# Scores of two heads issued together, behind transposes and values, in a two-layer attention trunk

## What is computed

```python
def _fox_attention(...):       # 16 heads of 64
    for i in range(S // 128):
        s = q[lo:hi] @ k[:hi].T * scale + (c[lo:hi, None] - c[None, :hi])
        p = softmax(where(causal, s, NEG_INF))
        out = p @ v[:hi]
def _dilated_group(q, k, v, window, dilation):   # (128,1), (512,4), (2048,16), 16 heads each
    s = where(mask, q @ k.T * scale, NEG_INF)
    m = max(s); p = exp(s - m); den = sum(p)
    return (p / den) @ v, m + log(den)
# merged: softmax over the three groups' m + log(den)
```

## Time and profile before

| | us |
|---|---|
| median of 3 runs | 1691.82 (1689.79 to 1691.88) |
| span of the profiled execution | 1690.7 |
| TensorE matmul busy | 1670.5 (99%) |
| weight loads busy | 1393.1 (82%) |
| VectorE busy | 811.6 (48%) |
| ScalarE busy | 598.7 (35%) |
| GpSimd busy | 359.3 (21%) |
| scores (L515), 512 instructions | 125.3 |

### The profile page before, as it was taken

How to read it: one execution, slowest core, us unless ns; L and a number is a source line. 1 busy time by engine, 2 the same in 40 slices (tenths; PEclk the granted TensorE clock), 3 DMA queues, 4 the chain that set the end, 5 groups by cost and what they waited for, 6 DMA issues and landing times.

```text
span 1690.7 us, 21646 instructions
## 1 busy us (share of the span) xinstructions
PE 1670.5 (99%) x8066; PEld 1393.1 (82%) x8066; DVE 811.6 (48%) x1388; ACT 598.7 (35%) x1068; POOL 359.3 (21%) x534
## 2 busy tenths in 40 slices
PE   7999999999999999999999999999999999999999
PEld 6777767888888888999988889998877888888887
DVE  4455556444443444434546565554646443534342
ACT  5433332442323233434344333343333432323240
POOL 3412200050000000444437354433712000000000
PEclk9999999999999999999999999999999999999999
DMA  5211110323232323332222312122222232323222
GB/s 165 88 50 38 46 43 1 100 88 111 76 111 87 112 77 111 118 94 63 74 64 63 126 51 67 58 75 63 63 102 88 75 112 84 102 87 105 94 91 84
DMA packets 77554, 139.81 MB, mean 83 GB/s; under 512 B 12192, under 2 KB 12192, under 8 KB 77216
## 3 DMA queue, kind: packets, MB, share of 16 engines
q1 hardware_dynamic: 75280, 134.51, 24.8%
q10 hardware_dynamic: 2192, 4.20, 0.7%
HBM read 132.33 MB, written 6.36 MB: 82 GB/s over the span
## 4 chain that ended last, share of the span: by engine, by line
PE 93%; POOL 3%; DVE 1%; ACT 1%; SPq 1%; issue 1%; DMA 0%; ACTq 0%; POOLq 0%; DVEq 0%
PE ps L461 75%; PE ps L515 7%; PE ps L543 5%; PE ps L529 3%; PE ps L555 2%; PE ps L492 1%; POOL qrs L1321 1%; POOL qss L1320 1%; PE ps L512 1%; ACT w_h L774 0%; DVE qss L1011 0%; DVE qn L1026 0%; PE ps L514 0%; ACT sq L812 0%; DMA w_raw<-in_fox_w_in 0%
## 5 line engine op out<-in xcount | busy, mean ns | idle before, releaser
L461 PE MATMUL ps<-w_h,act_h 128*128 128x512 f32 x768 | 317.5, 413 | 6.8 <-DVE w_l L985 3.4
L461 PE MATMUL ps<-w_h,act_l 128*128 128x512 f32 x768 | 306.5, 399 | 0.0
L461 PE MATMUL ps<-w_l,act_h 128*128 128x512 f32 x768 | 305.9, 398 | 0.0
L774 ACT ACTIVATE w_h<-w_raw,gain_t 128x512 fp32r<-128x512 f32 x316 | 209.9, 717 | 151.0 <-PE ps L461 105.4
L985 DVE SCALAR_TENSOR_TENSOR w_l<-w_raw,gain_t,w_h 128x512 fp32r<-128x512 f32 x316 | 226.9, 760 | 56.7 <-ACT w_h L774 56.7
L461 PE MATMUL ps<-w_h,hid_h 128*128 128x512 f32 x640 | 252.0, 394 | 0.6 <-DVE hid_l L993 0.5
L461 PE MATMUL ps<-w_l,hid_h 128*128 128x512 f32 x640 | 249.6, 390 | 0.0
L461 PE MATMUL ps<-w_h,hid_l 128*128 128x512 f32 x640 | 249.2, 389 | 0.0
L461 PEld LDWEIGHTS ps<-w_h,act_h 128*128 128x128 f32 x768 | 192.2, 250 | 25.0 <-issue 8.4
L461 PEld LDWEIGHTS ps<-w_l,act_h 128*128 128x128 f32 x768 | 192.2, 250 | 16.1 <-issue 0.7
L461 PEld LDWEIGHTS ps<-w_h,act_l 128*128 128x128 f32 x768 | 193.2, 252 | 13.5
(11 more groups left out here) (150 smaller groups left out, 2009.7 us busy)
## 6 DMA issues: line engine op xcount, KB each, us to landing
w_raw<-in_mlp_w SPq DMA_DIRECT2D x128, 512.0 KB, 3.6
w_raw<-in_dil_w_in SPq DMA_DIRECT2D x72, 512.0 KB, 3.5
w_raw<-in_fox_w_in SPq DMA_DIRECT2D x22, 512.0 KB, 3.5
w_raw<-in_fox_w_out SPq DMA_DIRECT2D x8, 512.0 KB, 3.6
w_raw<-in_dil_w_out SPq DMA_DIRECT2D x8, 512.0 KB, 3.6
acc_kept<-acc SPq DMA_DIRECT2D x2, 1056.0 KB, 6.3
o_sb<-acc_kept SPq DMA_DIRECT2D x2, 1056.0 KB, 5.1
x_sb<-in_x SPq DMA_DIRECT2D x4, 512.0 KB, 8.4
```

The source lines that it names most:

```text
L461: return mm(ps_out, lhs[i], rhs[j], start=(k == 0 and term == 0), stop=(k == KT - 1 and term == 2))
L774: last = fn(w_h[:, u % WR, j, :], raw(u)[:, j, :], ACT.Copy, scale=gain_t[:, norm, k:k + 1])
```

## The change

The ticks of a set now go by pairs of heads: bank 0 of the even head, bank 0 of the odd head, bank 1 of the even head, and so on. The scores of both heads of a pair are issued together, in the even tick, the even head on rows 0 to 63 into `ps_s[0]`, the odd one on rows 64 to 127 into `ps_s[1]`, segment by segment in turn, with all presets ahead of them. They stand behind `turn_probs` and `values` in the tick and no longer ahead of them. They wait for the exponentials of all ticks before. As two heads now share `o_ps`, the output of a bank is taken out in every tick (VectorE's `output` reads only that bank's query tiles), and values wait for the output of the tick before in every tick. The merge waits by ticks, and two small buffers are split.

```diff
@@ ticks_of
-    return [(h, i, i == len(banks) - 1) for h in range(HS) for i in range(len(banks))]
+    return [(2 * pair + odd, i, i == len(banks) - 1)
+            for pair in range(HS // 2) for i in range(len(banks)) for odd in range(2)]
+def new_slot(s, h):
+    return HS * sum(SETS[i][0] in (2, 0) for i in range(s)) + h
@@
-        rden = sb("rden", [P, 2, NT])
+        rden = sb("rden", [P, 4, NT])
@@ scores
-                rows = slice(HD * (h % 2), HD * (h % 2) + HD)
                 if a >= 2:
-                    pe.wait_ge(exp_done, a - 1)
-                col = 0
-                for q, k0, nk in SCORE_BANKS[kind][i]:
-                    ...
-                last.then_inc(s_full, 1)
+                    pe.wait_ge(exp_done, a)
+                h0, i, _ = ticks_of(s)[a - TICK0[s]]
+                segs = SCORE_BANKS[kind][i]
+                cols = [P * sum(nk for _, _, nk in segs[:j]) for j in range(len(segs))]
+                preset = kind == "fox" or mask_on_pe(s)
+                for odd in range(2):
+                    for j, (_, k0, nk) in enumerate(segs):
+                        dst = ps_s[odd][:, cols[j]:cols[j] + nk * P]
+                        if kind == "fox":
+                            hh = HS * half + h0 + odd
+                            mm(dst, pick[:, hh:hh + 1].broadcast_to([P, P]), c_parts[:, k0 * P:(k0 + nk) * P], start=j == 0, stop=False)
+                        elif preset:
+                            mm(dst, ident_b[:, :], banded[:, 256 - nk * P:256], start=j == 0, stop=False)
+                for j, (q, k0, nk) in enumerate(segs):
+                    for odd in range(2):
+                        rows = slice(HD * odd, HD * odd + HD)
+                        done = mm(ps_s[odd][:, cols[j]:cols[j] + nk * P], qT[s % 2][rows, h0 // 2, q * P:(q + 1) * P],
+                                  kT[s % 2][rows, h0 // 2, k0 * P:(k0 + nk) * P], start=not preset, stop=not preset or j == len(segs) - 1)
+                        if j == len(segs) - 1:
+                            done.then_inc(s_full, 1)
@@ values
-                if i == 0 and HS * s + h > 0:
-                    pe.wait_ge(o_done, HS * s + h)
+                if a >= 1:
+                    pe.wait_ge(o_done, a)
@@ step, TensorE
-                        if a < nt:
-                            scores(attend, t0 + a)
                         if 2 <= a <= nt + 1:
                             turn_probs(attend, t0 + a - 2)
                         if 3 <= a <= nt + 2:
                             values(attend, t0 + a - 3)
+                        if a < nt and a % 2 == 0:
+                            scores(attend, t0 + a)
@@ output, VectorE
-                if not last_bank:
-                    return
+                tiles = [q for q, _, _ in SCORE_BANKS[kind][i]]
+                span = slice(tiles[0], tiles[-1] + 1, max(1, (tiles[-1] - tiles[0]) // max(1, len(tiles) - 1)))
+                n = len(tiles)
                 dve.wait_ge(pv_done, a + 1)
                 if kind == "fox":
-                    link(v.reciprocal(rden[:, 0, :], o_ps[:, :, own_one(h)]))
-                    v.tensor_tensor(..., rden[:, 0, :]..., ALU.mult).then_inc(o_done, 1)
+                    link(v.reciprocal(rden[:, 0, span], o_ps[:, span, own_one(h)]))
+                    v.tensor_tensor(..., rden[:, 0, span]..., ALU.mult).then_inc(o_done, 1)
...
-                    m = evacuated[0]
-                    if m >= 2:
+                    m = new_slot(s, h)
+                    if m >= 2 and i == 0:
                         dve.wait_ge(merged, m - 1)
-                    v.tensor_copy(o_ring[:, m % 2, :, 0:VC], o_ps[:, :, 0:VC]).then_inc(o_done, 1)
+                    v.tensor_copy(o_ring[:, m % 2, span, 0:VC], o_ps[:, span, 0:VC]).then_inc(o_done, 1)
@@ merge, GpSimd
-                pool.wait_ge(o_done, HS * s + h + 1)
+                pool.wait_ge(o_done, a + 1)
```

More of the change, by code:

```diff
@@ L501, in scores @@
                 kind, half = SETS[s]
-                h, i, _ = ticks_of(s)[a - TICK0[s]]
-                rows = slice(HD * (h % 2), HD * (h % 2) + HD)
                 if a >= 2:
-                    pe.wait_ge(exp_done, a - 1)
-                col = 0
-                for q, k0, nk in SCORE_BANKS[kind][i]:
[L508 to L517, removed]
@@ L576, in step @@
                             if t == 0:
-                                pe.wait_ge(o_done if attend == 1 else normed, HS)
+                                pe.wait_ge(*((o_done, TICK0[1]) if attend == 1 else (normed, HS)))
                             prepare(1 if attend == 1 else 4, 0, t)
@@ L657, in out_projection @@
                 if prep == 1:
-                    pe.wait_ge(o_done, 2 * HS)
+                    pe.wait_ge(o_done, TICK0[2])
                 else:
@@ L1082, in factor_args @@
                             dve.wait_ge(acc_in, 16 * (half + 1))
-                        other = both = o_sb[:, :, (HS * half + h) // 2, VP + h % 2]
+                        other = o_sb[:, :, (HS * half + h) // 2, VP + h % 2]
                     if kind == 2:
@@ L1088, in factor_args @@
                     else:
-                        link(v.tensor_tensor(rden[:, 0, :], mine, other, ALU.min))
-                        v.tensor_tensor(e_arg[:, m % 4, 0, :], rden[:, 0, :], other, ALU.subtract)
-                        v.tensor_tensor(e_arg[:, m % 4, 1, :], rden[:, 0, :], mine, ALU.subtract).then_inc(earg_done, 1)
+                        both = rden[:, 2 + h % 2, :]
+                        link(v.tensor_tensor(both, mine, other, ALU.min))
+                        v.tensor_tensor(e_arg[:, m % 4, 0, :], both, other, ALU.subtract)
+                        v.tensor_tensor(e_arg[:, m % 4, 1, :], both, mine, ALU.subtract).then_inc(earg_done, 1)
                     merges[0] += 1
@@ L1099, in probs_back @@
                 v.tensor_copy(pT_sb[:, a % 2, 0:w], ps_p[a % 2][:, 0:w]).then_inc(pt_done, 1)
-            evacuated = [0]
             def output(s, a):
                 kind, half = SETS[s]
-                h, _, last_bank = ticks_of(s)[a - TICK0[s]]
-                if not last_bank:
-                    return
+                h, i, _ = ticks_of(s)[a - TICK0[s]]
+                tiles = [q for q, _, _ in SCORE_BANKS[kind][i]]
+                span = slice(tiles[0], tiles[-1] + 1, max(1, (tiles[-1] - tiles[0]) // max(1, len(tiles) - 1)))
+                n = len(tiles)
                 dve.wait_ge(pv_done, a + 1)
                 if kind == "fox":
-                    link(v.reciprocal(rden[:, 0, :], o_ps[:, :, own_one(h)]))
-                    v.tensor_tensor(o_sb[:, :, (HS * half + h) // 2, value_cols(h)], o_ps[:, :, own_values(h)],
-                                    rden[:, 0, :].unsqueeze(2).broadcast_to([P, NT, HD]), ALU.mult).then_inc(o_done, 1)
+                    link(v.reciprocal(rden[:, 0, span], o_ps[:, span, own_one(h)]))
+                    v.tensor_tensor(o_sb[:, span, (HS * half + h) // 2, value_cols(h)], o_ps[:, span, own_values(h)],
+                                    rden[:, 0, span].unsqueeze(2).broadcast_to([P, n, HD]), ALU.mult).then_inc(o_done, 1)
                 elif kind == 1:
@@ L1121, in output @@
                 else:
-                    m = evacuated[0]
-                    if m >= 2:
+                    m = new_slot(s, h)
+                    if m >= 2 and i == 0:
                         dve.wait_ge(merged, m - 1)
-                    v.tensor_copy(o_ring[:, m % 2, :, 0:VC], o_ps[:, :, 0:VC]).then_inc(o_done, 1)
-                    evacuated[0] += 1
+                    v.tensor_copy(o_ring[:, m % 2, span, 0:VC], o_ps[:, span, 0:VC]).then_inc(o_done, 1)
             def normalise(s, h):
```

## The result

The changed kernel takes 1716.17 us (median of 4 runs, 1714.70 to 1717.04) beside 1691.85 for the kernel before on the same chip: ratio 1.0151, 95% interval 1.0136 to 1.0165. It is 24 us slower; the forecast was 1678.5, and the time lies above the upper end of the stated range, 1706.

The account below looks back on a forecast made before the run. The matrix engine, busy 99% of the span, was taken as the bound. Terms -16.3+7.5+2.5-3.4-3.5=-13.2 us from a 1690.7 us profile (runs' median 1691.8) gave 1678.6, said as 1678.5; range 1672 to 1706.

Parts of the forecast that it names:

- the overlap: Score products on the two row halves run side by side, a dilated pair taking 9 slots, not 16; chance 0.42.
- the slot of lag: One extra score slot per pair of heads, 0.32, 0.22 or 0.43 us beside the FoX projection, taken off the gain.
- The four dilated steps: Sets of kinds 1 and 2: 1.08 us gained per pair over 16 pairs, one not kept, so -16.3 us.
- step 5,4: Kind 0 attention with projection: eight pairs gain 7.0 us, late norms in ticks 4 and 14 lose 2.2 and 1.3; -3.5.
- Loads take turns: Rival for score products: streams on the two halves overlap but weight loads do not; 1693 us, chance 0.32.
- no overlap: Rival for score products: the halves never run together and only switches are saved; 1704 us, chance 0.23.
- the colder clock: Rival: idling in attention-only steps drops the clock, doubling the rounds' matrix share; some +38 us, chance 0.03.
- FoX alone: FoX attention without projection: nine pairs +10.5 us, first two pairs -2, tail gains 1; sum +7.5.
- set 7: Set 7's attention without projection: five rounds +6.1 us, carried pairs -2, tail -1.6; sum +2.5.
- the closed round: Attention alone: VectorE's maxima, copies and outputs, then values and next scores, set each two-tick pace; FoX banks total 18.2 us.
- the tail: End of each attention-only step: FoX gains 1 us because the last head's scores are ready early; set 7 gains 1.6.
- step 1,0: FoX attention beside projection: twelve pairs take 102.7 us against 106.1, three of them slowed by late norms; -3.4.

Follow-up runs that it names:

- the filler: The changed kernel plus eleven unused 256-column products before values in each odd tick from 8 on of both attention-only steps; 1697.99 us.
- the norm last: The changed kernel with VectorE's q/k norm in set 0 moved behind maximum, copy and output; 1701.88 us.
- scores first: The changed kernel with the pair's scores ahead of transposes and values in their tick; 1659.13 us.
- heads in turn: New form in sets 2 to 6 only (1667.99 us), changed so all even-head scores are issued before the odd head's; 1674.28 us.

## Why the prediction was wrong

**Right: the overlap.** Both halves run side by side with their loads, the forecast's own case, and 8 slots per pair, not the 9 put down: no trace shows the slot of lag. The four dilated steps gained 19.0 where 16.3 was said, step 5,4 4.2 where 3.5 was. "Loads take turns" and "no overlap" are both out.

**Wrong: a chance of 0.03 for the colder clock.** This is the step that failed. The argument was that "the idle pieces are under 3 us each and work stands between". They were: 1.27, 0.46 and 1.57 us in the 8 us before 262.6, the longest in the step 1.81, and the clock fell all the same, for 47.8 of the 96.1 us of FoX alone and 37.5 of the 78.0 of set 7's. The engine was busy for 79.5 of the 96.1 us, much of it at half speed. The rival's price was sound per round: 25.4 us for three cold rounds (9.32, 8.44, 7.59) against 18.3 warm ones with the filler is 2.3 each, where 2.7 was said; 38 in all was too much, as not all rounds were cold. Measured with the filler: at least 20.9 us, by estimate 27 (see the sum below). Without it the change would have taken some 1689 to 1695 us, inside the stated range and about as long as the kernel before, where 1678.5 was forecast; so the clock is the larger part of the miss and not all of it.

The trace of the kernel before already spoke against the argument. The longest wait for qn, 2.0 us, is a single one in the first projection, behind dense work without a gap:

```profile
26.37 0.53 PE L461 MATMUL ps<-w_h,act_h 128*128 128x512 f32 x1 [1.99 <-DVE qn L1026]
```

The granted clock is at 1.2 GHz from 26.6 to 30.1 us there, the only such stretch within the span.

**Right in sum, by luck in part: the closed round.** Its three banks were put at 6.42, 6.08 and 5.70 us, sum 18.2; with the clock held up they measured 6.89, 5.77 and 5.66, sum 18.3. For set 7's five rounds 34.1 was said, and 34.0 measured (5.99 and 7.6 in turn for most, where 6.6 and 7.1 was said). VectorE does set the pace, as was said: waits for its outputs remain in every round. But single rounds are off by 0.5 us up and 0.3 down, and by 0.6 down and 0.5 up, and the sums come out because these cancel. One term was misread: the handover from 263.95 to 263.99 is 0.04 us and not 0.06.

**Mis-sized: what lies around the rounds.** With the filler, FoX alone is 13.8 us over before, where 7.5 was said, and set 7 6.8, where 2.5 was. In FoX the two pairs with carried dense terms gained 1.0 and not 2, the tail lost 1.5 instead of gaining 1, and the nine rounds from the fifth tick on took 57.5 us and not 54.6. In set 7 the tail lost 2.5 where a gain of 1.6 was said. Much of this is not the sum's error. Two fillers lie on the path in each tail, 2.3 us of it by estimate; less these, FoX's tail gains 0.8, near what was said, and set 7's loses 0.2. And 2.5 of the 2.9 us by which the nine rounds are longer are in the first two, before the filler keeps the clock up (6.54 and 8.55 against 5.66 and 6.89). Each of these two also holds four transposes of finished heads, 0.44 us, which stand in the kernel before too and which three times 18.2 leaves out; the other 1.6 fit the low clock in them. What is left as mis-sized is some 4.3 us: the carried pairs of FoX, these transposes, the tail of set 7, and little else.

**Wrong: step 1,0.** The round of norm, copy and output was seen, and its three pair periods nearly so: 10.9, 10.2 and 10.1 said; 10.91, 10.69 and 11.02 measured from the first load of a pair's presets to that of the next, each with a wait of 2.7 to 3.1 us. From first maximum to first maximum, as the prediction counted them, they are 12.9, 11.3 and 12.5, partly since the presets and scores behind two of the waits run at the low clock. Four things were left out. The fourth norm, at tick 22, was put at nothing since it "has no scores behind it", but values stand behind it too, and waited 2.96 us. Odd ticks have waits of their own, 0.58, 0.60, 1.31 and 0.09 us: an odd tick holds no scores any more and is short. With three of the four long waits the clock was low, for 13.7 us in all, worth some 5, an estimate from the run with the norm last. And the matrix work fell by more than the 10.8 us said: with the norm last the step without its waits is 105.1, 13.7 under before. The slot of lag per pair (0.32, 0.22, 0.43), some 3.9 us over the twelve pairs, was taken off and isn't there. The fourth wait 3.0, the odd ticks 2.6, the clock 5, and the three long waits 1.3 above the 7.4 that the three periods held, less 2.9 of matrix work, come to the 9.1 that were missing.

**What would show it.** The prediction expected one wait for o_sb in every even tick of the FoX step without projection. The waits are there, but the long ones lie in the odd ticks (1.81, 1.27, 1.57 us at 248.7, 255.9, 262.1). It also read 3.3 us as the longest wait of a dense product for VectorE; the same list has 3.4, once, for w_l, before the attention starts. Nothing in the sum hangs on that.

**The sum.** Of the 37.8 us between forecast and result, the clock in the attention-only steps has at least 20.9, step 1,0 has 9.1, and 10.6 lie in the pairs and tails around the rounds as measured with the filler. Of these 10.6, 4.7 are fillers on the path and 1.6 the slowing of the first two rounds, so that by estimate the clock has 27.2 and the rest 4.3. The dilated steps, step 5,4 and the start give back 2.7.

That the change put pairs last costs 57 us; the pairs in the old place gain 31. Why scores first lose so little (15.0 us of waits for outputs, and 6.6 for ScalarE's exponentials) is read from the timelines and not shown, since no run varied the cover alone: they are 1 to 1.5 us of work between the last tick's dense products and the values, just where VectorE needs time, and their maximum can begin that much earlier.

## What to carry to other kernels

Halves of the array that can run side by side are worth having, but an order on the matrix engine is also a timetable for the engine that serves it: put the work that others wait for first (57 us here), and keep what waits for a third engine (the norm) at the end of a queue, behind what the matrix engine needs at once (14 us in one step here). Where a change makes the matrix engine wait again and again in a stretch that had no waits, count with the low clock even if no single wait is long, and price a round at both clocks. Reading the trace by stretches from set to set, warm and cold apart, showed in one table what the total hid.

## What the runs showed of the hardware

- Two fp32 products on row halves 0 to 63 and 64 to 127 start 5 to 7 ns apart, their loads of 128 columns too: sixteen in 1.09 us, eight before.
- A product on the free half starts ahead of three products that stand before it in the program (heads in turn: the odd head's first beside the even head's fifth of eight, or beside its first of four).
- The granted clock went from 2.4 to 1.2 GHz after idle pieces of only 1.27, 0.46 and 1.57 us within 8 us, and stayed down for 30.7 us. With three of the four single waits of 2.7 to 3.1 us in step 1,0 it was low for 3.4 or 6.8 us.
- Eleven useless products per two ticks, in place of waits of 1.3 to 1.8 us, brought the clock back in most of both attention-only steps, and 18 us with it.
